# Running 256 context tokens through an even layer beside the sequence, with shared weight units

## What is computed

```python
def _even_mix(h, w_in, ...):
    a_val, a_glu, a_gate, b_val, b_gate = _split(h @ w_in, [512] * 5)
    u = a_val * sigmoid(a_glu)
    u = silu(_layernorm(_dwconv(u, a_conv_w) + a_conv_b, a_ln_g, a_ln_b))  # 31 taps
    y_a = (u @ a_pw_w + a_pw_b) * silu(a_gate)
    y_b = _fourier_mix(b_val, b_fw) * silu(b_gate)  # DFT over tokens and channels, real part
    return concatenate([y_a, y_b], axis=-1) @ w_out
x_new = x  + gt   * _even_mix(_pre(x,  e_norm, sh,   sc),   *args)
xc    = xc + gt_c * _even_mix(_pre(xc, e_norm, sh_c, sc_c), *args)
```

## Time and profile before

| what | value |
|---|---|
| runs, us | 3033.26 (median), 3033.35, 3023.74 |
| profiled execution, us | 3028.51 |
| its span, us | 3026.7 |
| mean granted TensorE clock | 0.923 |
| busy: PE, DVE, ACT, POOL | 86%, 49%, 19%, 27% of the span |
| moved by DMA | 195.8 MB, 65 GB/s mean |

### The profile page before, as it was taken

The page is one execution under the profiler, slowest core; times in us unless marked ns, Lnnn a source line. Parts: engine busy times, 40 slices in busy tenths (PEclk is TensorE's granted clock), DMA queues, the critical chain, the costliest instruction groups (busy, mean ns, idle before and its releaser), DMA issues.

```text
span 3026.7 us, 29623 instructions
## 1 busy us (share of the span) xinstructions
...
## 2 busy tenths in 40 slices
...
GB/s 256 91 169 61 18 16 8 8 84 84 63 111 84 80 90 96 97 84 84 94 52 49 66 67 57 49 49 26 49 35 49 28 47 43 42 104 14 1 15 69
DMA packets 248478, 195.76 MB, mean 65 GB/s; under 512 B 15184, under 2 KB 224720, under 8 KB 248368
## 3 DMA queue, kind: packets, MB, share of 16 engines
...
## 4 chain that ended last, share of the span: by engine, by line
PE 66%; DVE 21%; ACT 4%; issue 3%; PEld 2%; DMA 1%; POOL 1%; PEldq 1%; SPq 1%; ACTq 0%; DVEq 0%; POOLq 0%
PE G L1592 25%; PE G L303 22%; DVE eACC L1924 5%; DVE cACC L1924 3%; PE M L2441 3%; PE G L1029 2%; DVE WPT L2477 2%; PE M L2426 1%; PE G L2111 1%; PE G L2013 1%; PE M L2013 1%; PE M L1607 1%; PEld G L506 1%; PE M L393 1%; PE M L983 1%
## 5 line engine op out<-in xcount | busy, mean ns | idle before, releaser
L303 PE MATMUL G<-HH,WH 128*128 128x512 f32 (+1 forms) x1488 | 476.8, 389 | 82.1 <-DVE HL L427 39.0
L303 PE MATMUL G<-HL,WH 128*128 128x512 f32 (+1 forms) x1488 | 468.1, 383 | 0.0
L303 PE MATMUL G<-HH,WL 128*128 128x512 f32 (+1 forms) x1488 | 467.2, 382 | 0.0
L303 PEld LDWEIGHTS G<-HH,WH 128*128 128x128 f32 x1488 | 285.4, 193 | 156.4 <-issue 74.8
L278 POOL TENSOR_SCALAR WH<-RAW 128x1024 fp32r<-128x1024 f32 (+1 forms) x152 | 131.6, 866 | 922.9 <-PE G L1592 502.1
L266 POOL TENSOR_SCALAR WH<-RAW 128x1024 fp32r<-128x1024 f32 x92 | 101.8, 1106 | 945.5 <-PE G L303 732.8
L303 PEld LDWEIGHTS G<-HL,WH 128*128 128x128 f32 x1488 | 288.2, 194 | 57.9
L303 PEld LDWEIGHTS G<-HH,WL 128*128 128x128 f32 x1488 | 287.4, 193 | 57.9
L281 POOL TENSOR_TENSOR WL<-RAW,WH 128x1024 fp32r<-128x1024 f32 (+1 forms) x152 | 292.6, 1925 | 12.7
L269 POOL TENSOR_TENSOR WL<-RAW,WH 128x1024 fp32r<-128x1024 f32 x92 | 241.2, 2622 | 7.7
L1592 PE MATMUL G<-HH,WH 128*128 128x512 f32 x640 | 228.7, 406 | 14.2 <-POOL WL L281 9.4
...
## 6 DMA issues: line engine op xcount, KB each, us to landing
RAW<-in_w_ff SPq DMA_DIRECT2D x40, 512.0 KB, 4.0
...
RAW<-in_e_w_in SPq DMA_DIRECT2D x40, 512.0 KB, 3.7
...
WVEC<-in_w_ada SPq DMA_DIRECT2D x24, 512.0 KB, 4.4
FVEC<-in_e_w_mod SPq DMA_DIRECT2D x24, 512.0 KB, 3.9
FVEC<-in_o_w_mod SPq DMA_DIRECT2D x24, 512.0 KB, 3.8
RAW<-in_o_w_in SPq DMA_DIRECT2D x24, 512.0 KB, 3.8
```

The costliest lines, as they stand in the source:

```text
L303: m = pe.matmul(G[s][:, n * w:(n + 1) * w], part[s][:, k, :], moving[:, k, n * w:(n + 1) * w], start=(j == 0 and part is WH and moving is hi),
```

## The change

`even_layer` is gone and its body is written once for both inputs. The order is now `cin`, the context's norm and h (`cn`), the sequence's h (`en`), then one input, one Fourier, one half norm, one pointwise and one output stage in which every weight unit serves 1024 and 256 tokens: `gemm_unit` takes a `side` and adds, for each of its 24 weight tiles, a matmul of 256 columns into the PSUM tile M. `ckn` and `ckv` follow, then the odd layer. The context's h gets its own HHC and HLC. To make room, X is written to memory (SPILL) from `cin` on, its space is used for VB and GB, and XC is written out (CSPILL) at `en`; both are read back at `ean`, all by GpSimd's queue. The inversion of the sequence's norm moves to the start of `cn`. The cores of the parts:

```diff
-        for part, moving in ((WH, hi), (WH, lo), (WL, hi)):
+        for part, i in ((WH, 0), (WH, 1), (WL, 0)):
+            first, last = j == 0 and part is WH and i == 0, j == KT - 1 and part is WL
             for n in range(nt):
                 m = pe.matmul(G[s][:, n * w:(n + 1) * w], part[s][:, k, :],
-                              moving[:, k, n * w:(n + 1) * w], start=(j == 0 and part is WH and moving is hi),
-                              stop=(j == KT - 1 and part is WL))
+                              acts[i][:, k, n * w:(n + 1) * w], start=first, stop=last)
+            if side:
+                m = pe.matmul(M[s][:, 0:CTX], part[s][:, k, :], side[i][:, k, :], start=first, stop=last)
     m.then_inc(unit_done[s], 1)
-def lead_in(name, T, signal, tiles=range(KT), freed=None):
...
+        if side:
+            dve.wait_ge(moved, info("ean")["dma_end"])
         for f in range(KT):
-            if along:
-                ada_rows(dve, name, f)
-            add_gated(dve, u0 + f, f, T, X_, gate(f))
-            if along and f:
-                ada_add(dve, first_ada, f - 1)
+            unit_ready(dve, u0 + f)
+            if side:
+                dve.scalar_tensor_tensor(out=side[0][:, f, :], in0=M[f % 2][:, 0:CTX], scalar=side[1](f),
+                                         in1=side[0][:, f, :], op0=ALU.mult, op1=ALU.add)
+            dve.scalar_tensor_tensor(out=X_[:, f, :], in0=G[f % 2][:], scalar=gate(f), in1=X_[:, f, :],
+                                     op0=ALU.mult, op1=ALU.add).then_inc(unit_freed[f % 2], 1)
...
+        if begin_dve:
+            begin_dve(dve)
...
+        norm_stage(tag, X_, T, False, "eps2", dve_, act_, gathered=gathered, sq=sq, r=r, dmas=dmas,
+                   begin_dve=begin_dve)
     else:
...
-def even_layer(tag, X_, T, c, r_known=None):
-    rms_h(tag + "n", X_, T, 0, c, gathered=False, r_known=r_known)
-    w = T + 2 * PAD
...
+stage("cin", dict(act=cin_act, pe=cin_pe, dve=cin_dve), dmas=[(SPILL[:, f, :], X[:, f, :]) for f in range(KT)])
+def invert_er(dve):
+    dve.reciprocal(ER[:], ER[:]).then_inc(S("er"), 1)
+rms_h("cn", XC, CTX, 0, 1, gathered=False, high=HHC, low=HLC, begin_dve=invert_er)
+rms_h("en", X, SEQ, 0, 0, r_known=ER, dmas=[(CSPILL, XC[:])])
+VB, GB = at("VB", [P, 4, SEQ], F32, 0), at("GB", [P, 4, SEQ], F32, 16 * kb)
+VBC, GBC, GAC = [Z(n, [P, 4, CTX], F32, 4 * i) for i, n in enumerate(("VBC", "GBC", "GAC"))]
+GA = Z("GA", [P, 4, SEQ], F32, 12)
+ACC, ACCC = Z("ACC", [P, SEQ], F32, 28), Z("ACCC", [P, CTX], F32, 32)
+UC = Z("UC", [P, 4, CTX + 2 * PAD], F32, 52)
+U = Z("U", [P, 4, SEQ + 2 * PAD], F32, 57)
+SG, SGC = Z("SG", [P, SEQ], F32, 73.5), Z("SGC", [P, CTX], F32, 77.5)
...
+def conv(dve, a, b):
+    for q in range(a, b):
+        j, k = divmod(q, CONV_W)
+        wk = V[:, VEC["conv_w"] + j * CONV_W + k:VEC["conv_w"] + j * CONV_W + k + 1]
+        if k == 0:
+            dve.wait_ge(S("ein_u"), 1 + j + 1)
+            if j:
+                dve.wait_ge(S("ein_cv"), 2 * j)
+        for i, (u, acc, T) in enumerate(((U, ACC, SEQ), (UC, ACCC, CTX))):
+            tap = S(("ein_tap", "ein_ctap")[i])
+            if q:
+                dve.wait_ge(tap, q)
+            if k == 0:
+                dve.tensor_scalar(acc[:], u[:, j, k:k + T], wk, vec("conv_b", j), ALU.mult, ALU.add)\
+                   .then_inc(tap, 1)
+            else:
+                dve.scalar_tensor_tensor(out=acc[:], in0=u[:, j, k:k + T], scalar=wk, in1=acc[:], op0=ALU.mult,
+                                         op1=ALU.add).then_inc(tap, 1)
+        if k == CONV_W - 1:
+            for i, (u, acc, T) in enumerate(((U, ACC, SEQ), (UC, ACCC, CTX))):
+                dve.wait_ge(S(("ein_tap", "ein_ctap")[i]), q + 1)
+                dve.tensor_copy(u[:, j, 0:T], acc[:]).then_inc(S("ein_cv"), 1)
+def ein_dve(dve):
+    u0 = info("ein")["u0"]
+    dve.wait_ge(moved, info("en")["dma_end"])
+    for u, T in ((U, SEQ), (UC, CTX)):
+        dve.memset(u[:, :, 0:PAD], 0.0).then_inc(S("ein_pad"), 1)
+        dve.memset(u[:, :, PAD + T:2 * PAD + T], 0.0).then_inc(S("ein_pad"), 1)
+    dve.wait_ge(S("ein_pad"), 4)
+    dve.sem_inc(S("ein_u"), 1)
+    step = 0
+    for j in range(4):
+        unit_ready(dve, u0 + 2 * j + 1)
+        dve.wait_ge(unit_freed[0], u0 // 2 + j + 1)
+        dve.tensor_tensor(U[:, j, PAD:PAD + SEQ], G[1][:], SG[:], ALU.mult).then_inc(S("ein_m"), 1)
+        dve.tensor_tensor(UC[:, j, PAD:PAD + CTX], M[1][:, 0:CTX], SGC[:], ALU.mult).then_inc(S("ein_m"), 1)
+        dve.wait_ge(S("ein_m"), 2 * j + 2)
+        dve.sem_inc(S("ein_u"), 1)
+        dve.sem_inc(unit_freed[1], 1)
+        if j < 3:
+            conv(dve, step, step + 12)
+            step += 12
+    conv(dve, step, 4 * CONV_W)
+def ein_act(act):
+    u0 = info("ein")["u0"]
+    n = 0
+    for j in range(4):
+        unit_ready(act, u0 + 2 * j)
+        if j:
+            act.wait_ge(S("ein_u"), j + 1)
+        act.activation(SG[:], G[0][:], ACT.Sigmoid).then_inc(S("ein_a"), 1)
+        act.activation(SGC[:], M[0][:, 0:CTX], ACT.Sigmoid).then_inc(S("ein_a"), 1)
+        n += 2
+        act.wait_ge(S("ein_a"), n)
+        act.sem_inc(unit_freed[0], 1)
+    act.wait_ge(moved, info("en")["dma_end"])
...
+    for j in range(12):
+        U_ = u0 + 8 + j
+        unit_ready(act, U_)
+        f = ACT.Copy if j < 4 else ACT.Silu
+        act.activation((VB, GB, GA)[j // 4][:, j % 4, :], G[U_ % 2][:], f).then_inc(S("ein_a"), 1)
+        act.activation((VBC, GBC, GAC)[j // 4][:, j % 4, :], M[U_ % 2][:, 0:CTX], f).then_inc(S("ein_a"), 1)
+        n += 2
+        act.wait_ge(S("ein_a"), n)
+        act.sem_inc(unit_freed[U_ % 2], 1)
...
+stage("ein", dict(lead=lead_in("ein", SEQ, "en_lo", side=(HHC, HLC)), act=ein_act, dve=ein_dve,
+                  pe=lambda pe: gemm_pairs(pe, info("ein")["u0"], 10, SEQ, (HH, HL), led=True, side=(HHC, HLC))),
+      raw=[(1, lambda s, i, j=j: ein_src(2 * j + s)) for j in range(10)], units=20)
...
+    ones_sum(pe, M[0], SEQ, [AR])
+    ones_sum(pe, M[1], CTX, [ARC]).then_inc(S("ef_mean"), 1)
...
+    for t in range(N_DFT):
+        src, _, _, _, par, i, _ = dft_tile(t)
+        if t >= 2:
+            pe.wait_ge(S("ef_v"), 2 * (t - 1))
...
+        if t == NT:
+            pe.wait_ge(S("ef_ev"), 3)
...
+    act.activation(EVC[:], banks_c[0], ACT.Copy).then_inc(S("ef_ev"), 1)
+    act.wait_ge(S("ef_gate"), 5)
+    act.activation(HHC[:, 4:8, :], YBC[:], ACT.Copy).then_inc(S("ef_hi"), 1)
...
+    dve.wait_ge(S("ef_ev"), 5)
+    even, odd = banks_c[1].rearrange("p (g n) -> p g n", n=P), EVC[:].rearrange("p (g n) -> p g n", n=P)
+    dve.tensor_tensor(YBC[:, :, 0:P], even, odd, ALU.add).then_inc(S("ef_y"), 1)
+    dve.scalar_tensor_tensor(out=YBC[:, :, P:CTX], in0=even, scalar=-1.0, in1=odd, op0=ALU.mult, op1=ALU.add)\
+       .then_inc(S("ef_y"), 1)
+    dve.wait_ge(S("ef_y"), 10)
+    dve.tensor_tensor(YBC[:], YBC[:], GBC[:], ALU.mult).then_inc(S("ef_gate"), 1)
+    dve.wait_ge(S("ef_hi"), 5)
+    dve.tensor_tensor(HLC[:, 4:8, :], YBC[:], HHC[:, 4:8, :].bitcast(F32), ALU.subtract).then_inc(S("ef_lo"), 1)
...
+def ean_pe(pe):
+    ones_sum(pe, M[1], SEQ, [AR])
+    ones_sum(pe, M[0], CTX, [ARC]).then_inc(S("ea_var"), 1)
+def ean_dve(dve):
+    dve.wait_ge(S("ea_sd"), 1)
+    dve.reciprocal(AR[:], AR[:]).then_inc(S("ea_r"), 1)
+    dve.wait_ge(S("ea_sd"), 2)
+    dve.reciprocal(ARC[:], ARC[:]).then_inc(S("ea_r"), 1)
+    dve.wait_ge(S("ea_r"), 2)
+    for i, (u, r, _, T) in enumerate(sums_of):
+        for j in range(4):
+            dve.tensor_tensor(u[:, j, 0:T], u[:, j, 0:T], r[:], ALU.mult).then_inc(S("ea_xn"), 1)
+def ean_act(act):
...
+stage("ean", dict(act=ean_act, pe=ean_pe, dve=ean_dve),
+      dmas=[(XC[:], CSPILL)] + [(X[:, f, :], SPILL[:, f, :]) for f in range(KT)])
...
+        for k in range(4):
+            for n in range(2):
+                pe.matmul(G[j % 2][:, n * 512:(n + 1) * 512], RAW[j % 2][:, k, :],
+                          U[:, k, n * 512:(n + 1) * 512], start=(k == 0), stop=(k == 3))
+            m = pe.matmul(M[j % 2][:, 0:CTX], RAW[j % 2][:, k, :], UC[:, k, 0:CTX], start=(k == 0), stop=(k == 3))
+        m.then_inc(raw_used[j % 2], 1)
...
+        for g, ps in ((GA[:, j, :], G[j % 2][:]), (GAC[:, j, :], M[j % 2][:, 0:CTX])):
+            dve.scalar_tensor_tensor(out=g, in0=ps, scalar=vec("pw_b", j), in1=g, op0=ALU.add, op1=ALU.mult)\
+               .then_inc(S("ep_g"), 1)
+        dve.wait_ge(S("ep_hi"), 2 * j + 2)
+        dve.tensor_tensor(HL[:, j, :], GA[:, j, :], HH[:, j, :].bitcast(F32), ALU.subtract)\
+           .then_inc(S("ep_part"), 1)
+        dve.tensor_tensor(HLC[:, j, :], GAC[:, j, :], HHC[:, j, :].bitcast(F32), ALU.subtract)\
+           .then_inc(S("ep_part"), 1)
+        dve.wait_ge(S("ep_part"), 2 * j + 2)
...
+out_stage("eout", A["e_w_out"], X, lambda f: MODE[:, 16 + f, 0:1], ("ep_lo", range(4), ("ep_g", 6)),
+          side=(XC, lambda f: MODE[:, 16 + f, 1:2], (HHC, HLC)))
...
-even_layer("c", XC, CTX, 1)
-rms_h("ckn", XC, CTX, 1, 1)
```

(71 more changed lines are left out.)

392 lines of the change are left out of this document (130 added, 262 removed).

## The result

| | before | after |
|---|---|---|
| median of the runs beside each other | 3032.06 us (4 runs) | 2981.93 us (4 runs, 2975.29 to 2987.89) |
| profiled execution | 3028.5 us | 2987.89 us (span 2986.1) |
| ratio after / before | | 0.984, 95% interval 0.9822 to 0.9858 |

What follows compares the result with a forecast made beforehand. No one engine was taken to bound the kernel, but a chain of stages, with VectorE's taps ending the input stage. Added 95.6 us less removed 207.0 gave net -111.4 from 3028.5, so 2917.1; predicted 2918 us, range 2898 to 2947.

Steps and rivals of the forecast that it cites:

- a unit of weights for both: Merged units: 24 added matmuls of 256 columns cost 2.8 us, making a unit 14.0 us; GpSimd's split stays far below.
- Rival 2: Input stage: GpSimd and VectorE shut each other out more, a split costing VectorE 3.4 us; 10 us more, 2928; chance 0.15.
- rival 3: Input stage: TensorE ends it at 267.7 us, losses per split being 2.0 us or less; 2913 us; chance 0.10.
- A pair at 1.60: Input stage: a sequence tap and a context tap, alternating on VectorE, together take 1.60 us.
- rival 1: Input stage: alternating the taps hides nothing, pairs take 1.84 us; VectorE's tail 21 us longer, 2939 us; chance 0.12.
- The loss per split: Input stage: each of 11 GpSimd weight splits beside the taps costs VectorE 2.5 us, 27.5 us in all.
- The h stage's +3.4: Sequence's h stage: 3.0 us for the weights' first two splits and 0.4 for the lead's last slice.
- The other terms: Later stages' growth: Fourier +9.3 us, norm of the convolved half +5.0, pointwise +9.7, output +20.0, second context norm +4.4.
- The returned X: Reload of 5.2 MB before the output stage's first gated add: costs 0, with 27 us of cover.
- The sign: Whole kernel: the change makes it faster, with chance 0.98; same 0.01, slower 0.01.

Runs made afterwards that it cites:

- e8_psum_again: The kernel of e4_psum unchanged, run again (context's accumulator in PSUM, against the changed kernel): median 2897.57 us, 0.9585 of before.
- e4_psum: Changed kernel, but the context's accumulator lies in PSUM, so every second tap has one input in SBUF only: median 2899.34 us, 0.957 of before.

## Why the prediction was wrong

1. **The step that failed** is in the paragraph on a unit of weights for both: "GpSimd's split of the weights, some 3.4 us for a unit, stays far below that". It lasts up to 38.6 us (36.24 + 2.34). The 3.4 us were read from taps that wait each for the one before: they repeat at 1.32 us and last 1.285, so each leaves 0.035 us free, and no WH of the two input stages of before lasts longer than 1.94 us. I used the alternation to take that gap away (1.20 + 0.40 = 1.60), and kept for GpSimd a price that had been measured with the gap in place. In its place the runs show waits of 31.6 to 35.2 us ahead of three splits, and 71.9 us of TensorE's time lost to them.
2. **The same in the rivals.** Rival 2 says that "the alternating taps leave no gap" and names the exclusive lock, but lets VectorE pay: 11 x 0.9 us. The runs show the other side. VectorE paid nothing during the long waits, and its last copy ended 254.0 us after the first matmul (1916.12 - 1662.13), earlier than the 272.3 I had; GpSimd paid up to 36 us at a time, and through it TensorE, which I had put 4.6 us short of the bound. The order of the engines in the stage was right only as long as GpSimd got in. The right rival would have been: the first half of a split waits for the end of a block of taps, three times, some 24 us each beyond what the unit under way covers. TensorE then ends the stage at 267.7 + 71.9 = 339.6 us in place of VectorE's 272.3, and the kernel takes 2917 + 67 = 2984.
3. **The sum without that step was good.** With GpSimd let in, the stretch of the norm and the input stage takes 303.3 us (one gap in eight) and 305.2 (one in four), against 300.8 forecast, and the kernel 2913 against 2917. With PSUM rival 3 comes true, TensorE ends the stage (forecast 267.7 us from its first matmul; measured in e8_psum_again 1908.43 - 1640.85 = 267.6, in e4_psum 266.1), at 2899 us where I had put 2913. VectorE's end lay at 265.5 us there (1906.30 - 1640.85), not at 272.3. The rest of the difference can't be split up: the early part of the kernel alone differs by 21 us between profiles, so that the agreement of the totals to a few us is in part luck.
4. **A pair at 1.60** was right (1.59), and rival 1's "waits already met cost nothing visible" holds for a wait on an instruction that ended before: one on the tap just before costs 0.18 us a pair, both together 0.38. Rival 1's 1.84 was too low for that case.
5. **The loss per split**, 2.5 us: 2.9 with two inputs in SBUF, 2.2 with every second tap on PSUM. The h stage's +3.4, of which 3.0 were the splits by the same loss, was 4.6.
6. **The other terms** hold within 3 us: Fourier 111.4 (forecast some 111), half norm 22.5 (24), pointwise 50.5 (53), output 105.0 (105), second context norm 18.0 (18.5). The returned X, in flight 8.6 us for a piece of 512 KB, is waited for by nobody: its last piece was issued at 2122.5, none took longer than 11.1 us, and the first gated add runs at 2192.
7. **The sign** was right, the range was not: on the slow side it took in prices for VectorE alone. (Its lower end, 2898, also lies 15 us under rival 3's 2913 and not the 8 us given there.) A case in which GpSimd's split grows past 14 us had no place in it, though the earlier trace rows showed that both sides pay when they meet (2.38 against 3.25 us).
